# FoX prompt attention run one query block further ahead, with two buffers for probabilities and turned copies, and the residual parked in DRAM during the mixers

## What is computed

```
def fox_prompt(q, k, v, logf):
    c = jnp.cumsum(logf, axis=1)
    ...
    def block(args):                      # one block of 128 queries, 8 blocks
        i, q_i, c_i = args
        s = jnp.einsum('bqhd,bkhd->bhqk', q_i, k) * scale
        s = s + (c_i[..., :, None] - c_keys[..., None, :])
        s = jnp.where(key_pos[None, :] <= qpos[:, None], s, -jnp.inf)
        p = jax.nn.softmax(s, axis=-1)
        return jnp.einsum('bhqk,bkhd->bqhd', p.astype(v.dtype), v)
```

## Time and profile before

| | us |
|---|---|
| median of 3 runs | 4746.04 (4736.3 to 4746.28) |
| the profiled execution, device time | 4743.37 |
| its span in the profile | 4741.8 |
| PE busy in the span | 4221.7 (89%) |
| DVE, ACT, POOL busy | 1401.9, 738.0, 330.6 |
| mean granted PE clock | 0.919 of full speed |

### The profile page before, as it was taken

How to read it: one execution, slowest core, us unless ns; L and a number is a source line. 1 busy time by engine, 2 the same in 40 slices (tenths; PEclk the granted TensorE clock), 3 DMA queues, 4 the chain that set the end, 5 groups by cost and what they waited for, 6 DMA issues and landing times.

```text
span 4741.8 us, 58317 instructions
## 1 busy us (share of the span) xinstructions
PE 4221.7 (89%) x21598; PEld 3142.5 (66%) x21598; DVE 1401.9 (30%) x3031; ACT 738.0 (16%) x1345; POOL 330.6 (7%) x563
## 2 busy tenths in 40 slices
PE   7888798977788999999998888889677989999998
PEld 4677576755455888876656775768454568888665
DVE  3345214024323333310034441220443143333001
ACT  1222101034200111100022220110442011111000
POOL 1000002211110000000000000021112000000000
PEclk9989695989888999999999887879897989999998
DMA  3300110112341111121113001001126211111212
GB/s 80 23 0 0 33 32 10 34 42 80 123 158 54 36 44 44 49 69 37 43 32 14 0 0 42 22 20 24 56 71 231 75 35 43 44 44 42 71 36 67
DMA packets 273319, 232.32 MB, mean 49 GB/s; under 512 B 24124, under 2 KB 237184, under 8 KB 271888
## 3 DMA queue, kind: packets, MB, share of 16 engines
q1 hardware_dynamic: 243776, 142.66, 11.9%
q0 software_dynamic: 29392, 87.62, 5.7%
HBM read 206.05 MB, written 24.18 MB: 49 GB/s over the span
## 4 chain that ended last, share of the span: by engine, by line
PE 82%; DVE 7%; issue 5%; ACT 3%; DMA 1%; another core or an unknown queue 0%; DVEq 0%; POOL 0%; POOLq 0%; ACTq 0%; SPq 0%
PE ps L859 78%; PE ps L863 4%; ACT wd L2462 1%; DVE hT L1580 1%; DMA big<-in_x_prompt 0%; ACT wd L2470 0%; DVE big L1801 0%; ACT big L2439 0%; DMA wd<-in_state_rwkv 0%; DVE sil L1573 0%; DVE big L1809 0%; DMA big<-in_cache_fox_k 0%; DVE big L1769 0%; DVE big L1762 0%
## 5 line engine op out<-in xcount | busy, mean ns | idle before, releaser
L859 PE MATMUL ps<-hT,ring 128*128 128x352 f32 (+1 forms) x3712 | 1063.8, 440 | 58.8 <-DVE xT L2161 40.1
L859 PEld LDWEIGHTS ps<-hT,ring 128*128 128x128 f32 x3712 | 712.6, 193 | 373.2 <-DVE xT L2161 42.2
L859 PE MATMUL ps<-big,wd 128*128 128x352 f32 (+3 forms) x2576 | 702.9, 432 | 11.2 <-DVE big L1771 7.6
L859 PEld LDWEIGHTS ps<-big,wd 128*128 128x128 f32 (+2 forms) x2576 | 457.0, 190 | 251.9 <-issue 17.5
L859 PE MATMUL ps<-xT,ring 128*128 128x264 f32 x1408 | 342.3, 386 | 0.1
L859 PE MATMUL ps<-big 128*128 128x128 f32 (+5 forms) x1520 | 264.1, 346 | 54.4 <-POOL big L701 14.8
L859 PEld LDWEIGHTS ps<-xT,ring 128*128 128x128 f32 x1408 | 267.4, 190 | 46.5 <-DVE xT L2178 0.9
L859 PEld LDWEIGHTS ps<-big 128*128 128x128 f32 (+3 forms) x1520 | 212.9, 225 | 93.3 <-issue 23.8
L863 PE MATMUL ps<-ident,big 128*128 128x128 f32 (+5 forms) x998 | 175.7, 327 | 108.6 <-ACT big L2325 28.1
L859 PE MATMUL ps<-ring,hT 128*128 128x128 f32 (+1 forms) x2304 | 261.5, 275 | 0.0
L859 PEld LDWEIGHTS ps<-ring,hT 128*128 128x128 f32 (+1 forms) x2304 | 256.9, 183 | 5.2 <-issue 2.4
(11 more groups left out here) (371 smaller groups left out, 3935.2 us busy)
## 6 DMA issues: line engine op xcount, KB each, us to landing
ring<-in_w_in SPq DMA_DIRECT2D x60, 512.0 KB, 3.8
ring<-in_w_gate SPq DMA_DIRECT2D x44, 512.0 KB, 4.1
ring<-in_w_up SPq DMA_DIRECT2D x44, 512.0 KB, 4.0
wd<-in_w_down SPq DMA_DIRECT2D x16, 1408.0 KB, 7.2
big<-in_cache_fox_k SPq DMA_DIRECT2D x64, 256.0 KB, 5.5
big<-in_cache_fox_k POOLq DMA_DIRECT2D x64, 256.0 KB, 5.6
big<-in_cache_fox_v SPq DMA_DIRECT2D x64, 256.0 KB, 4.9
big<-in_cache_fox_v POOLq DMA_DIRECT2D x64, 256.0 KB, 4.9
```

What stands on the lines that cost most here:

```text
L859: return pe.matmul(out, lhsT, rhs, start=start, stop=stop, skip_group_check=True)
```

## The change

The loop over `pp` is gone: the four pairs `u` stand written out in each layer. `sp_` and `ptt` get two whole buffers each, used by even and odd blocks; the second ones lie in `xT`. Therefore `xT` is stored to `xkeep` after the first norm of the layer and loaded again after the last cached values of the samples have been asked for, both by POOL; DVE waits for the second before it adds the first result of `w_out`. The order on the engines is new, S(i+2) standing behind P(i) and V(i-1) for every block, and the first scores of the next pair standing ahead of rt:

```diff
-        sp_ = region((wdf, 0), 2, T)
-        ptt = region((wdf, 2 * T), 2, NTT, P)
+        xfree = xT[:, :, :].rearrange("p a b -> p (a b)")
+        sp_ = [region((wdf, 0), 2, T), region((xfree, 0), 2, T)]
+        ptt = [region((wdf, 2 * T), 2, NTT, P), region((xfree, 2 * T), 2, NTT, P)]
...
-        scores_after = {0: 2, 1: 3, 3: 4, 4: 5, 5: 6, 6: 7}
+        ahead = lambda i: i + 2 if i + 2 < NTT else None
...
+                    pool.wait_ge(n_dve, NRM_DVE.at(2 * l, f"h{KT - 1}"))
+                    pool.sem_inc(passed, 1)
+                    for k in range(KT):
+                        pool.dma_start(xkeep[k], xT[:, k, :]).then_inc(x_out, 16)
                     pool.wait_ge(*evac_at(l, 6))
...
                         half("cache_fox_v", value_in, g, a, range(4))
 
+                pool.wait_ge(x_out, l * (32 * KT) + 16 * KT)
+                pool.sem_inc(passed, 1)
+                for k in range(KT):
+                    pool.dma_start(xT[:, k, :], xkeep[k]).then_inc(x_back, 16)
+                pool.wait_ge(x_back, l * (32 * KT) + 16 * KT)
                 for k in range(KT):
                     pool.wait_ge(*evac_at(l, J_OUT + k))
...
+                scores(0, 0)
+                scores(0, 1)
+                for u in PAIRS_Q:
+                    pe.wait_ge(fp_act, FP_ACT.at(l, f"{u - 1}R") if u else FP_ACT.at(l - 1, "3R"))
+                    for i in range(NTT):
+                        last = tr(ps[:, 4 + i // 4, P * (i % 4):P * (i % 4) + P], ktp[u % 2][:, P * i:P * i + P])
+                    FP_PE.mark(last, fp_pe, f"{u}ko")
+                    for i in QB:
+                        probs(u, i)
+                        if i:
+                            values(u, i - 1)
+                        if ahead(i):
+                            scores(u, ahead(i))
+                    if u < 3:
+                        scores(u + 1, 0)
+                        scores(u + 1, 1)
+                    pe.wait_ge(*fd(f"{u}r"))
+                    pe.wait_ge(*fa(f"{u}{piece_names(NTT - 1, 0)[-1]}"))
...
+                    values(u, NTT - 1)
+                    pe.wait_ge(*fd(f"{u}rt"))
...
+                lowest(0, 0)
+                lowest(0, 1)
+                for u in PAIRS_Q:
+                    for i in QB:
+                        turned(u, i)
+                        if ahead(i):
+                            lowest(u, ahead(i))
+                    on(fa(f"{u}e{NTT - 1}1"))
+                    fm(v.reciprocal(rrec, rsum), f"{u}r")
+                    if u < 3:
+                        lowest(u + 1, 0)
...
+                on((x_back, l * (32 * KT) + 16 * KT))
+                v.sem_inc(passed, 1)
                 for j in range(J_OUT, J_FF):
...
+                prob(0, 0)
+                for u in PAIRS_Q:
+                    on((ko_free, l * 4 + (u + 1)))
+                    on(fpp(f"{u}ko"))
+                    fm(a.copy(ko.rearrange("p i t -> p (i t)"), ps[:, 4:6, :].rearrange("p a b -> p (a b)")), f"{u}ko")
+                    prob(u, 1)
+                    for i in QB:
+                        turned(u, i)
+                        if ahead(i):
+                            prob(u, ahead(i))
+                    if u < 3:
+                        prob(u + 1, 0)
+                    on(fpp(f"{u}R"))
+                    fm(a.copy(rbc, ps[:, 4:6, :].rearrange("p a b -> p (a b)")), f"{u}R")
```

More of the change, by code:

```diff
@@ L1408, in _, with scores @@
-                pe.wait_ge(fp_dve, FP_DVE.at(l * 2 + 1, "1o"))
+                FP_PE.start()
+                fd = lambda n: (fp_dve, FP_DVE.at(l, n))
+                fa = lambda n: (fp_act, FP_ACT.at(l, n))
+                def scores(u, i):
+                    if i == 0:
+                        pe.wait_ge(fp_pool, FP_POOL.at(l * 4 + u, "k"))
+                        if u:
+                            pe.wait_ge(*fd(f"{u - 1}d{NTT - 1}1"))
+                    elif i in (2, 3):
+                        pe.wait_ge(*fd(f"{u}d{i - 2}1"))
+                    elif i >= 4:
+                        pe.wait_ge(*fd(f"{u}d{i - 1}1"))
+                    w = P * (i + 1)
+                    bank = lambda hh, a: 2 * hh + (i % 2 if i < 4 else a // 512)
+                    for a in range(0, w, 512):
+                        e = min(a + 512, w)
+                        for hh in range(2):
+                            r = slice(HD * hh, HD * hh + HD)
+                            mm(ps[:, bank(hh, a), 0:e - a], qtp[u % 2][r, P * i:P * i + P], ktp[u % 2][r, a:e], True, e < w)
+                    for hh in range(2):
+                        last = mm(ps[:, bank(hh, w - P), P * (i % 4):P * (i % 4) + P], ident[:, :], fmask, False, True)
+                    FP_PE.mark(last, fp_pe, f"{u}S{i}")
@@ new lines, in probs @@
+                def probs(u, i):
+                    for n, (hh, c) in enumerate(pieces(i)):
+                        x = first_piece(i) + n
+                        acts = [f"{u}e{i}{hh}"]
+                        if x == 0:
+                            acts.append(f"{u}ko")
+                        if x >= 2:
+                            hb, cb = (pieces(i) if n >= 2 else pieces(i - 1))[n - 2]
+                            copied = f"{u}pt{i if n >= 2 else i - 1}{hb}{cb}"
+                            if x % 2:
+                                pe.wait_ge(*fd(copied))
+                            else:
+                                acts.append(copied)
+                        pe.wait_ge(*fa(max(acts, key=FP_ACT.names.index)))
+                        for k in range(4 * c, min(4 * c + 4, i + 1)):
+                            last = tr(ps[:, 4 + x % 2, P * (k % 4):P * (k % 4) + P], sp_[i % 2][:, hh, P * k:P * k + P])
+                        FP_PE.mark(last, fp_pe, f"{u}pt{i}{hh}{c}")
@@ new lines, in values @@
+                def values(u, i):
+                    if i == 0:
+                        pe.wait_ge(fp_dve, FP_DVE.at(l, f"{u - 1}o") if u else FP_DVE.at(l - 1, "3o"))
+                    pe.wait_ge(*fa(f"{u}{piece_names(i, 0)[-1]}"))
+                    pe.wait_ge(*fd(f"{u}{piece_names(i, 1)[-1]}"))
+                    for k in range(i + 1):
+                        for hh in range(2):
+                            r = slice(HD * hh, HD * hh + HD)
+                            last = mm(ps[r, 6 + i // 4, P * (i % 4):P * (i % 4) + P], vp[u % 2][:, k, r], ptt[i % 2][:, hh, k, :], k == 0, k == i)
+                    FP_PE.mark(last, fp_pe, f"{u}V{i}")
@@ L1409, in _ @@
+                pe.wait_ge(fp_dve, FP_DVE.at(l, "3o"))
                 pe.wait_ge(past_in, l * NPAST + NPAST)
@@ L2062, in _ @@
                 FS_DVE.start()
-                on((fp_dve, FP_DVE.at(l * 2 + 1, "1o")))
+                on((fp_dve, FP_DVE.at(l, "3o")))
                 fsm_(v.memset(qb, 0.0), "qz")
@@ L2213, in _ @@
                 pair_of_tiles(PAIRS - 1, last=True)
[L2214 removed]
+                on((x_back, l * (32 * KT) + 32 * KT))
                 v.sem_inc(passed, 1)
@@ new lines, in _, with prob @@
+                FP_ACT.start()
+                log_exp()
+                fm = lambda ins, n: FP_ACT.mark(ins, fp_act, n)
+                fd = lambda n: (fp_dve, FP_DVE.at(l, n))
+                fpp = lambda n: (fp_pe, FP_PE.at(l, n))
+                def prob(u, i):
+                    w = P * (i + 1)
+                    for hh in range(2):
+                        s = 2 * i + hh
+                        on(fd(f"{u}d{i}{hh}"))
+                        fm(act(sp_[i % 2][:, hh, 0:w], sp_[i % 2][:, hh, 0:w], ACT.Exp, scale=-1.0, bias=mn[:, s:s + 1], accum_out=rsum[:, s:s + 1]), f"{u}e{i}{hh}")
```

218 lines of the change are left out of this document (60 added, 158 removed).

## The result

| | before | after |
|---|---|---|
| median of the runs beside each other, us | 4741.17 (4734.65 to 4746.28, 4 runs) | 4789.52 (4781.96 to 4796.08, 4 runs) |
| ratio, 95% interval | | 1.0103 [1.0087, 1.0119] |
| the profiled execution, its span, us | 4743.37, 4741.8 | 4781.96, 4780.4 |
| mean granted PE clock | 0.919 | 0.912 |

The change makes the kernel 1% slower, 48 us by the medians and 38.6 by the two profiled executions. I cut both spans at five marks that both traces have: the store of the RWKV shift rows, DVE's first step on a pair's queries, the last copy of R, and the first product with `w_out`.

A forecast was written before the change was run, and what follows sets the result against it. A pair was taken as a chain through PE, DVE and ACT with no engine full. 4743.4 + 14 (order) + 22 (clock) + 3 (residual's traffic) = 4782 us, range 4748 to 4815.

The forecast's parts named there:

- The front of a block and G: FoX blocks 5 to 7: time from the end of S(i) to the second head's pieces, 3.73, 4.08 and 4.44 us.
- The order term at full clock: FoX pairs: the new order costs +2.0 us a pair, +1.2 for a layer's last, +14 in all (+7 to +24).
- the boundary's loss: From S7 to the next pair's P0: 21.3 us against 15.98 now, +5.3 a pair.
- The clock term: FoX: 24 joined PE idle gaps of 3.0 to 3.5 us, 16 clock falls at 1.4 us, +22 (0 to +50).
- rival 2: FoX: the clock falls at every gap and at the boundary, 2 us each, 4820 us; chance 0.15.
- The residual's traffic: Store and reload: the reload delays the first `w_out` block by 1.5 us a layer, +3 (0 to 5 a layer).
- the written-out pairs: Loop over `pp` gone: counted as 0, at most 0.3 us a layer to be had.
- Rivals 1, 3 and 4: FoX: clock holds, 4760 (0.18); boundary loses less than front gains, 4727 (0.06); pair nets out, 4747 (0.09).

The follow-up runs named there:

- deep: Changed kernel with ACT copying a block's pieces before the next block's exponential, and DVE's copies (blocks from 4) between the next block's two heads: ratio 0.9899 to before.
- filled: Changed kernel with 8, 9 and 10 unread matmuls before the second head's pieces of blocks 4, 5 and 6, every wait left: ratio 1.0001 to before.
- deep_bound: Changed kernel with both the deep and bound edits: 4669.97 us, ratio 0.9842 to before; 0.9845 when run again.
- bound: Changed kernel with only the boundary undone, the next pair's first scores S0' and S1' behind R again: 4780.42 us, ratio 1.0076 to before.
- old_order: Changed kernel with the engine orders of the kernel before, only e1 kept after ko: 4729.45 us, ratio 0.9963 to before.
- after_again: Changed kernel run once more, unaltered, for the scatter: 4794.87 us, ratio 1.0095 to before.
- before_park: Kernel before with only the residual's store and reload added: 4739.09 us, ratio 0.9985.
- no_park: Changed kernel without the residual's store and reload (outputs behind the mixers left wrong): 4795.44 us, ratio 1.0097 to before.
- unrolled: Kernel before with its four pairs written out and nothing else changed: 4735.99 us, ratio 0.9978.
- split: Changed kernel with V(i-1) put between the two heads' pieces of P(i) for i >= 4: 4748.43 us, ratio 0.9999 to before.

## Why the prediction was right, and where its steps were off

The forecast was 4782 and slower; the profiled execution took 4781.96 and the median is 4789.5. That the two agree to a microsecond is luck: term by term the forecast is less good than it looks.

**The front of a block and G: right.** G5, G6 and G7 were put at 3.73, 4.08 and 4.44 and are 3.82, 4.17 and 4.53 (1107.58 to 1111.40, 1117.01 to 1121.18, 1127.33 to 1131.86). The mechanism, ACT's copy behind e(i+1), is shown by deep.

**The order term at full clock: right.** From filled: S5 to S6, 1096.94 to 1104.73, is 7.79 (7.80 predicted), S6 to S7 8.68 (8.68). P0 to the end of S5 is 1080.31 to 1092.15 = 11.84 in deep_bound, where it is at full clock and in the new order's sequence on PE; bound, which keeps the change's order on ACT and DVE there too, has 11.85 (1085.36 to 1097.21). Predicted were 12.2. S7 to S0' 11.12 (11.0) and on to the next P0 10.39 (10.3) in filled. Together 49.8 for a pair (49.9), so +1.9 instead of +2.0, and the sum of +14 stands. Of the boundary's loss bound undoes only the early S0' and S1', with the clock that they cost: 9 to 13 us by the ratios. The rest of it, what stands behind S7, is shown by filled's lengths alone.

**The clock term: mechanism right, size wrong, +49 instead of +22.** The step that failed is the count. I let two in three of 24 gaps bring a fall; 22 did. Only the second gap of the last pair of each layer held, kernel after, timeline of PE: the gap, V4, S7.
```profile
1236.95 0.88 PE L876 MATMUL ps<-ident,xT 128*128 128x128 f32 x6 [3.35 <-ACT xT L2485]
1237.76 1.31 PE L872 MATMUL ps<-wd,ring 128*64 128x128 f32 x20
1239.00 1.99 PE L872 MATMUL ps<-ring 64*128 64x512 f32 x8
```
S7 takes 1.99 here and 3.08 behind the same gap in pair two. The price of a fall was near: the two stretches that are 7.79 and 8.68 at full clock are 9.43 (1107.58 to 1117.01) and 10.32 (1117.01 to 1127.33) in the kernel after, 1.64 each where I took 1.4; the others cost 1.35 to 1.64, but for two that cost 2.5. All gaps together are 36.6 us. And I had left the boundary to rival 2: P0 to the end of S5 takes 14.27 in pair two (1093.31 to 1107.58), 2.4 over 11.84, and between 1.7 and 2.9 in each of the eight pairs (the first of a layer too, with no R ahead of it), 19.5 in all. From 36.6 + 19.5 = 56 go the falls of before: 4.5 and 1.3 in the first pairs of the two layers, and 1.6 in the last pair of layer 0, which takes 46.03 from its ko copy to its copy of R where that of layer 1 takes 44.42. Kernel before, timeline of PE, P4's second head and S5 there:
```profile
1206.83 0.76 PE L863 MATMUL ps<-ident,wd 128*128 128x128 f32 x5 [0.57 <-ACT wd L2470]
1207.53 2.67 PE L859 MATMUL ps<-ring 64*128 64x512 f32 x8
```
S5 takes 2.67 instead of the 1.56 of the earlier trace rows, behind idle times of only 1.00 and 0.57 us. That leaves +49. With the order's 14 it is 63, against 61.9 measured for the stage and 63 to 65 between old_order and after_again. By mechanism, then, rival 2 (every gap and the boundary) is what happens, all but two gaps; its price of 2 us a fall was too high. The section "HAM oscillation — how this bites in real kernels" of the Trainium skill's "TensorE: Matmul & The Clock Gate" says that each burst behind a long wait starts slow again: the trace agrees, 22 times of 24, and I gave the one row that held too much weight against it.

**The residual's traffic: +3 predicted, nothing measured.** The wait for `w_out` grew as it should, to 5.89 and 6.76 (4.6 to 9 predicted), but before_park and no_park show no cost in the time, down to a gain of 0.15%. The value was inside the bounds of 0 to 10.

**What I had at nothing and was not: the written-out pairs.** The prediction let the loop's edge be worth 0.3 us a layer at most. By unrolled the pairs written out are worth 5 to 17 us (0.9965 to 0.999), it seems outside the stage; through what is not shown. In the profiled executions the untouched stretches gave back 23 us, much of it scatter. This, and the clock term short by 27, made the total come out near: two errors of opposite sign, of which neither was foreseen.

**Rivals 1, 3 and 4** fall: the clock did not hold; the boundary lost 5.5 at full clock (21.5 against 15.98), and the pair did not net out.

## What to carry to other kernels

Running one step further ahead gains nothing if the step that frees a PSUM bank stands behind the new step in a third engine's program: reorder every engine's queue with the first, short copies ahead of long work for the next block, and the extra buffers pay (here from +1.0% to -1.6%, of which the pairs written out alone bring 0.2%). When a chain leaves PE waiting in one piece of three microseconds or more, price each such piece with a fall of the clock, some 1.6 us here, and not a share of them; shorter ones can bring a fall too. A control that adds work that nobody reads and leaves the waits alone tells clock from order in one run.

## What was unexpected of the hardware

- The clock fell behind an idle time of 2.09 us (split, 1160.80), and in the kernel before behind 1.00 and 0.57 (1206.83 above). It held behind 2.14 (split, 1177.04), and behind 3.35 us twice (1236.95 above, and the same group at 3581.91 in layer 1). The length of one gap does not decide it; what lay before differs, and what exactly does was not isolated.
- Eight to ten small products in a gap of 3.1 to 3.6 us, leaving 1.33 to 1.37 idle, kept the clock there: 0.96 instead of 0.85 for pair two, and 20 us a layer.
- Behind R, whose products have two rows, and two waits of 1.10 each around ko, PE ran at its lower level in the kernel after: P0 and S2 took 0.69 and 1.65 instead of 0.44 and 0.92 at each boundary. With S0' and S1' between R and ko, as in bound and deep_bound, P0 and S2 behind R were at full clock, but a slow stretch could fall on S1' and ko instead: in deep_bound's third pair they take 1.23 and 1.37 instead of 0.70 and 1.04 (1158.37 and 1160.54), and the pair 42.1 instead of 40.6.
- 4.3 MB more each way between SBUF and DRAM (eight transfers of 528 KB), in each layer, beside the weight stream cost nothing that shows in the time (before_park 0.9985 [0.9972, 0.9998]), though the next wait for weights grew.
